# mLSTM row logits and mask by TensorE products, the maximum as a bias, the state's decay on ScalarE, and a phase barrier that TensorE passes

## The reference, cut to what matters

```python
bcum = cumsum(fc)
dmat = where(tril, bcum[t] - bcum[s] + it[s], -inf)
m_t  = maximum(bcum + m_prev, dmat.max(axis=-1))
w    = exp(dmat - m_t);  wqk = w * (q @ k.T);  a = exp(bcum + m_prev - m_t)
num  = wqk @ v + a * (c_prev @ q);  den = wqk.sum(-1) + a * (n_prev . q)
h    = num / maximum(abs(den), exp(-m_t))
m_new = maximum(b_last + m_prev, (b_last - bcum + it).max(-1))
decay = exp(b_last + m_prev - m_new);  ws = exp(b_last - bcum + it - m_new)
c_new = decay * c_prev + (ws * v).T @ k
```

## Time and profile before

| | |
|---|---|
| profiled execution, its own time | 3641.28 us |
| its span, first to last instruction | 3639.6 us |
| median of three runs | 3638.76 us |
| mean granted TensorE clock, share of 2.4 GHz | 0.937 |
| TensorE matmul busy | 3242.0 us (89%) |
| VectorE / ScalarE / GpSimd busy | 1779.0 / 1031.9 / 409.0 us |

### The profile page before, as it was taken

The page is one execution under the profiler, slowest core; times in us unless marked ns, Lnnn a source line. Parts: engine busy times, 40 slices in busy tenths (PEclk is TensorE's granted clock), DMA queues, the critical chain, the costliest instruction groups (busy, mean ns, idle before and its releaser), DMA issues. The chain is left out here.

```text
span 3639.6 us, 45789 instructions
## 1 busy us (share of the span) xinstructions
PE 3242.0 (89%) x17846; PEld 2901.8 (80%) x17846; DVE 1779.0 (49%) x3262; ACT 1031.9 (28%) x1632; POOL 409.0 (11%) x286
## 2 busy tenths in 40 slices
PE   6988899979999989599999868889979999879997
PEld 5978888868899789599999858667767797657875
DVE  6656445432346765764211374645523387443234
ACT  2221224323222442211211122124423324332221
POOL 0001200100010010321022020010000110121011
PEclk6999999979999999799999979999989999989998
DMA  5411320211042013342221233131221331232322
GB/s 189 156 38 37 86 93 24 83 51 53 24 163 87 24 70 116 108 124 75 71 69 44 90 122 95 44 107 59 70 64 53 114 124 35 95 114 83 108 81 98
DMA packets 332305, 303.73 MB, mean 83 GB/s; under 512 B 39822, under 2 KB 309852, under 8 KB 330204
## 3 DMA queue, kind: packets, MB, share of 16 engines
q1 hardware_dynamic: 315406, 229.74, 21.1%
q10 hardware_dynamic: 16718, 71.52, 5.3%
HBM read 266.47 MB, written 34.34 MB: 83 GB/s over the span
## 5 line engine op out<-in xcount | busy, mean ns | idle before, releaser
L741 PE MATMUL ps<-u_hi,w_hi 128*128 128x384 f32 (+1 forms) x2352 | 690.1, 355 | 61.4 <-ACTq L410 19.1
L741 PE MATMUL ps<-u_hi,w_lo 128*128 128x384 f32 (+1 forms) x2352 | 684.3, 353 | 0.0
L741 PE MATMUL ps<-u_lo,w_hi 128*128 128x384 f32 (+1 forms) x2352 | 683.9, 353 | 0.0
L1529 DVE TENSOR_TENSOR w_lo<-w_raw,w_hi 128x2048 fp32r<-128x2048 f32 x145 | 357.4, 2465 | 482.2 <-ACT w_hi L1135 481.0
L741 PEld LDWEIGHTS ps<-u_hi,w_hi 128*128 128x128 f32 x2352 | 435.6, 192 | 95.4 <-issue 43.4
L741 PEld LDWEIGHTS ps<-u_lo,w_hi 128*128 128x128 f32 x2352 | 437.5, 192 | 22.5
L741 PEld LDWEIGHTS ps<-u_hi,w_lo 128*128 128x128 f32 x2352 | 437.0, 191 | 22.8
L1135 ACT ACTIVATE w_hi<-w_raw 128x2048 fp32r<-128x2048 f32 x145 | 277.4, 1913 | 515.1 <-PE ps L741 295.3
L833 PE MATMUL ps<-u_hi,w_hi 128*128 128x384 f32 (+1 forms) x816 | 320.4, 393 | 4.5 <-ACT space L1278 3.5
L833 PE MATMUL ps<-u_hi,w_lo 128*128 128x384 f32 (+1 forms) x816 | 298.0, 365 | 0.0
L833 PE MATMUL ps<-u_lo,w_hi 128*128 128x384 f32 (+1 forms) x816 | 295.3, 362 | 0.0
(11 more groups left out here) (232 smaller groups left out, 4538.2 us busy)
## 6 DMA issues: line engine op xcount, KB each, us to landing
w_raw<-in_w_in SPq DMA_DIRECT2D x288, 256.0 KB, 4.1
space<-in_w_mod SPq DMA_DIRECT2D x48, 1024.0 KB, 5.5
w_raw<-in_w_gate_up SPq DMA_DIRECT2D x176, 256.0 KB, 4.0
w_raw<-in_w_down SPq DMA_DIRECT2D x96, 192.0 KB, 2.8
w_raw<-in_w_branch SPq DMA_DIRECT2D x64, 256.0 KB, 3.5
h_scratch<-space ACTq DMA_DIRECT2D x4, 3072.0 KB, 9.3
space<-h_scratch ACTq DMA_DIRECT2D x4, 3072.0 KB, 10.3
m_scratch<-space ACTq DMA_DIRECT2D x3, 3072.0 KB, 10.0
```

The lines of the kernel that those rows point to most:

```text
L741: last = nc.tensor.matmul(ps[:, 2 * (t % 2) + b, 0:a1 - a0], wv[w][:, k, j * P:(j + 1) * P], xx[:, k, a0:a1], start=(k == 0 and w == 0 and ...
L1529: V.tensor_tensor(w_lo[slot][:, :], w_raw[slot][:, :], w_hi[slot][:, :].bitcast(F32), ALU.subtract).then_inc(w_lo_done, 1)
```

## The change

`rows(k+1)` is now made of one bf16 product (identity by mask, 512 columns) and, for each head, a product whose stationary operand is the logit column broadcast to 128 columns and whose moving operand is the identity. Steps that want no output make no rows. The chunk's unmasked maximum, before a reduction over each step's rows, is made once a layer in `prep_b` by a transpose, a reduction, a diagonal and a product. ScalarE takes the exponential per head straight from PSUM with the negated maximum as bias. The decay of the state is four ScalarE copies with a scale. The key scale 128^-0.5 moves into the copy that moves b_k out of PSUM. At a phase's end the other three engines wait for each other and for TensorE, while TensorE waits only where the next phase is no `gemm`; a `down` group's products wait for the split hidden tiles instead.

```diff
             def end(self):
                 self.n += 1
-                self.eng.drain().then_inc(phase_end, 1)
-                self.eng.wait_ge(phase_end, 4 * self.n)
+                self.eng.drain().then_inc(others_end, 1)
+                self.eng.wait_ge(others_end, 3 * self.n)
+                self.eng.wait_ge(pe_end, self.n)
+            def end_products(self, onward):
+                self.n += 1
+                self.eng.drain().then_inc(pe_end, 1)
+                if not onward:
+                    self.eng.wait_ge(others_end, 3 * self.n)
...
                 for g in groups:
+                    if g.name.startswith("down"):
+                        pe.wait_ge(hid_split, g.h0)
...
-                def rows(k):
-                    i = n.lstm + k
-                    pe.wait_ge(m_diag, i + 1)
-                    if i:
-                        pe.wait_ge(m_arg, i)
-                    nc.tensor.matmul(ps[:, 0, :], ones[:, :], b_diag[i % 2].rearrange("p h n -> p (h n)"), start=True,
-                                     stop=True).then_inc(m_rows, 1)
+                def rows(k, w):
+                    d, ch, want, _ = steps[k]
+                    if not want:
+                        return
+                    if w:
+                        pe.wait_ge(m_w, w)
+                    nc.tensor.matmul(ps[:, 0, :], ident_b[:, :],
+                                     mask_b[:, d, :].unsqueeze(1).to_broadcast([P, HEADS, P]), start=True, stop=False)
+                    for h in range(HEADS):
+                        last = nc.tensor.matmul(ps[:, 0, h * P:(h + 1) * P],
+                                                r_in[:, d, ch, h:h + 1].to_broadcast([P, P]), ident[:, :],
+                                                start=False, stop=h == HEADS - 1)
+                    last.then_inc(m_rows, 1)
...
+                        pe.wait_ge(r_ready, 2 * l + 1)
+                        nc.tensor.transpose(ps[0:48, 2, 0:P], r_in[:, :].rearrange("p d t h -> p (d t h)"),
+                                            ident[:, :]).then_inc(r_turned, 1)
+                        pe.wait_ge(r_ready, 2 * l + 2)
+                        nc.tensor.matmul(ps[:, 3, 0:48], ones[0:48, :], r_diag[0:48, :], start=True,
+                                         stop=True).then_inc(r_spread, 1)
...
-                        act.wait_ge(m_dm, n.lstm_e + 1)
-                        A(b_w[i % 2], b_dm[i % 2], ACT.Exp).then_inc(m_w, 1)
+                        act.wait_ge(m_neg, n.lstm_e + 1)
+                        for h in range(HEADS):
+                            last = A(b_w[i % 2][:, h, :], ps[:, 0, h * P:(h + 1) * P], ACT.Exp,
+                                     bias=b_neg[i % 2][:, h:h + 1])
+                        last.then_inc(m_w, 1)
...
+                def decay(k):
+                    i, d = n.lstm + k, steps[k][0]
+                    act.wait_ge(m_ex, i + 1)
+                    if steps[k][2]:
+                        act.wait_ge(m_prod, n.lstm_w)
+                    if i:
+                        act.wait_ge(m_state, i)
+                    for h in range(HEADS):
+                        last = A(c_st[:, d, h, :], c_st[:, d, h, :], ACT.Copy, scale=b_ex[:, i % 2, 3, h:h + 1])
+                    last.then_inc(m_decay, 1)
...
                     fill_split(k)
+                    decay(k)
                     if counts[k]:
...
-                def diagonal(k):
-                    d, ch, _, _ = steps[k]
-                    V.tensor_tensor(b_diag[(n.lstm + k) % 2], ident[:, :].unsqueeze(1).to_broadcast([P, HEADS, P]),
-                                    bc(r_in[:, d, ch, :], P), ALU.mult).then_inc(m_diag, 1)
...
-                    dve.wait_ge(m_rows, i + 1)
-                    own.did(V.reduce_max(b_max[:, 0, :], rows, AX))
+                    own.wait()
                     if want:
-                        own.did(V.tensor_tensor(dm, rows, mask[:, d, :].unsqueeze(1).to_broadcast([P, HEADS, P]),
-                                                ALU.add))
-                        own.wait()
-                        own.did(V.reduce_max(b_max[:, 1, :], dm, AX))
+                        dve.wait_ge(m_rows, n.lstm_m + 1)
+                        own.did(V.reduce_max(b_max[:, 1, :], ps[:, 0, :].rearrange("p (h n) -> p h n", h=HEADS), AX))
+                        n.lstm_m += 1
+                    own.did(V.tensor_tensor(b_max[:, 3, :], r_max4[:, d, ch, :], m, ALU.max))
...
-                        V.tensor_tensor(dm, dm, bc(b_max[:, 2, :], P), ALU.subtract).then_inc(m_dm, 1)
+                        V.tensor_scalar(b_neg[i % 2], b_max[:, 2, :], -1.0, None, ALU.mult).then_inc(m_neg, 1)
...
-                    own.did(V.tensor_scalar(b_ws[:, :], ex[:, 2, :], HD ** -0.5, None, ALU.mult))
-                    own.wait()
...
-                    own.did(V.tensor_tensor(c_st[:, d], c_st[:, d], bc(ex[:, 3, :], HD + 1), ALU.mult))
...
+                    dve.wait_ge(m_decay, i + 1)
                     dve.wait_ge(m_dc, i + 1)
```

More of the change, by code:

```diff
@@ L327, in build @@
         B_TWO = words(8, 6 * BW).rearrange("p (r s h n) -> p r s h n", r=3, s=2, h=HEADS)
-        b_diag, b_dm, b_w = ([B_TWO[:, i, j] for j in range(2)] for i in range(3))
+        b_w = [B_TWO[:, 2, j] for j in range(2)]
+        b_small = words(8, 4 * BW)
+        r_top, r_diag, r_max = b_small[:, 0:1], b_small[:, 64:112], b_small[:, 128:176]
+        r_max4 = r_max.rearrange("p (d t h) -> p d t h", d=2, t=NT)
+        b_neg = [b_small[:, 192 + HEADS * j:192 + HEADS * (j + 1)] for j in range(2)]
         B_TMP = words(26, 2 * BW + 2 * HEADS * (HD + 1))
@@ L380, in build @@
         m_stored, m_loaded, gate_sig = sem("m_stored"), sem("m_loaded"), sem("gate_sig")
-        m_diag, m_rows, m_scores, m_keys = sem("m_diag"), sem("m_rows"), sem("m_scores"), sem("m_keys")
-        m_dm, m_w, m_arg, m_ex = sem("m_dm"), sem("m_w"), sem("m_arg"), sem("m_ex")
+        r_ready, r_turned, r_spread = sem("r_ready"), sem("r_turned"), sem("r_spread")
+        m_rows, m_scores, m_keys, m_decay = sem("m_rows"), sem("m_scores"), sem("m_keys"), sem("m_decay")
+        m_neg, m_w, m_arg, m_ex = sem("m_neg"), sem("m_w"), sem("m_arg"), sem("m_ex")
         m_wqk, m_wt, m_wts, m_kws = sem("m_wqk"), sem("m_wt"), sem("m_wts"), sem("m_kws")
@@ L989, in keys @@
                     last.then_inc(m_keys, 1)
-                rows(0)
+                rows(0, n.lstm_w)
                 scores(0)
@@ L998, in mlstm @@
                     if more:
-                        rows(k + 1)
+                        rows(k + 1, w + want)
                     fill(k, 0)
@@ L1118, in _ @@
                             n.tr += 1
-                ph.end()
+                onward = kind == "gemm" and index + 1 < len(phases) and phases[index + 1][0] == "gemm"
+                ph.end_products(onward)
         @block.scalar
@@ L1168, in gemm_unit @@
                         A(tile_at(dst_tile(g, it, s, j), g.lat), acc(t % 2, g.lat),
-                          ACT.Copy if g.kind == "copy" else ACT.Sigmoid).then_inc(acc_free[t % 2], 1)
+                          ACT.Copy if g.kind == "copy" else ACT.Sigmoid,
+                          scale=HD ** -0.5 if g.name == "b_k" else 1.0).then_inc(acc_free[t % 2], 1)
                     elif g.name in SQUARED:
@@ L1921, in maxima @@
                         own.did(V.tensor_tensor(b_max[:, 2, :], b_max[:, 1, :], m, ALU.max))
-                    own.did(V.tensor_tensor(b_max[:, 3, :], b_max[:, 0, :], m, ALU.max))
-                    own.wait()
-                    if want:
-                        V.tensor_tensor(dm, dm, bc(b_max[:, 2, :], P), ALU.subtract).then_inc(m_dm, 1)
+                        own.wait()
+                        V.tensor_scalar(b_neg[i % 2], b_max[:, 2, :], -1.0, None, ALU.mult).then_inc(m_neg, 1)
                         own.did(V.tensor_tensor(arg[:, 0, :], m, b_max[:, 2, :], ALU.subtract))
@@ L1939, in mlstm @@
                     weights, ex = b_w[i % 2].rearrange("p h n -> p (h n)"), b_ex[:, i % 2]
-                    if k + 1 < len(steps):
-                        diagonal(k + 1)
                     if want:
@@ L1944, in mlstm @@
                         dve.wait_ge(m_scores, w + 1)
-                        V.scalar_tensor_tensor(weights, ps[:, 1, :], HD ** -0.5, weights, ALU.mult,
-                                               ALU.mult).then_inc(m_wqk, 1)
+                        V.tensor_tensor(weights, ps[:, 1, :], weights, ALU.mult).then_inc(m_wqk, 1)
                     dve.wait_ge(m_ex, i + 1)
-                    own.did(V.tensor_scalar(b_ws[:, :], ex[:, 2, :], HD ** -0.5, None, ALU.mult))
-                    own.wait()
                     dve.wait_ge(m_keys, i + 1)
-                    V.tensor_tensor(b_kws, ps[:, 3, :].rearrange("p (h n) -> p h n", h=HEADS), bc(b_ws[:, :], P),
+                    V.tensor_tensor(b_kws, ps[:, 3, :].rearrange("p (h n) -> p h n", h=HEADS), bc(ex[:, 2, :], P),
```

(9 more changed lines are left out.)

12 lines of the change are left out of this document (6 added, 6 removed).

## The result

The changed kernel takes 3578.92 us (median of 4 runs, 3576.45 to 3582.47), against 3639.4 for the kernel before on the same chip (4 runs, 3634.82 to 3640.52): ratio 0.9836, 95% interval 0.9823 to 0.9848. It is 60.5 us faster, where 70 was forecast; the time lies inside the range, 9.9 us above the forecast of 3569. The two profiled executions are 3641.28 and 3579.07, 62.2 apart.

What follows compares the result with a forecast made beforehand. TensorE, busy nearly nine tenths of the span, was taken to bound the kernel. Savings of 18.7 + 22.5 + 15.7 + 13.0 = 69.9 us from 3641.3 gave 3571.4 profiled, about 3569 us median; range 3553 to 3598.

Steps and rivals of the forecast that it cites:

- The forecast case: Whole kernel: all summed gains arrive, 69.9 us saved, about 3569 us; chance 0.56.
- rows are dear: mLSTM row products on TensorE take 2.1 us a step instead of 1.04, losing 20 us: 3589; chance 0.08.
- ScalarE's queue becomes the bound: mLSTM steps: VectorE waits for late ScalarE decays ahead of the state's update, kernel slower, 3675 us; chance 0.02.
- the edit does more: Cheap rows (0.6 us), a short prep (1.6), no restart cost at barriers: 3557 us; chance 0.09.
- TensorE gives the barriers back: Dense phases: TensorE runs ahead but next weight splits are late, 15.7 + 7.9 us lost: 3593; chance 0.08.
- the clock does not come back: Short TensorE idle times, as in steps without fills, still lower its clock: 13 us lost, 3582; chance 0.15.
- the steps without fills: mLSTM layer 1, steps 4 and 9: weights' transposes still wait for VectorE, so gains are 0.9 and 1.1 us.
- a full step: mLSTM step: idle gap 1.87 us and L968's 0.97 go, new rows cost 1.04, net 1.80 us saved.
- layer 1, clock apart: Layer 1's mLSTM: start, steps and last step together save 22.5 us, without any clock gain.
- clock inside the mLSTM: Three falls of TensorE's clock in the two mLSTM layers, 1.7 us each, would go: 5.1 us.
- barriers, idle time: Fourteen TensorE waits between dense phases: ten shrink to 0.4 us each, four down places lose the barrier's hop; 15.7 us saved.
- clock at the barriers: After five of the ten barrier waits TensorE's lowered clock would no longer fall: 7.9 us saved.

Runs made afterwards that it cites:

- the mLSTM alone: The changed kernel with TensorE waiting at every barrier again, against the kernel before: 3597.57 us, ratio 0.9882.
- barrier alone: The kernel before with only the hunks that let TensorE pass the barriers, mLSTM as before: 3625.58 us, ratio 0.9954.
- the early diagonal: The kernel before with VectorE making the diagonal of step k+2 right behind the maxima of step k+1: 3606.08 us, ratio 0.9901.
- the down groups: The changed kernel with the first unit of each down group waiting for each hidden tile as it comes to it: 3559.36 us, ratio 0.9782.

## Why the prediction was right, and where its sum was off

**The forecast case came true.** Rows start without idle time behind the state's product, the ten waits are down to 0.3 each, and the kernel is 1.6% faster. Of the rivals, *rows are dear* fell (1.03 us a set), *ScalarE's queue becomes the bound* fell twice (decay back on VectorE, decay made 1.6 us later for 3.4 us in all), *the edit does more* fell, and *TensorE gives the barriers back* fell, but for d_q. What did happen is half of *the clock does not come back*: the 5.1 us inside the mLSTM came, most of the 7.9 at the barriers did not, and not because of the steps without fills that this rival named.

Term by term, against the two profiled executions (62.9 us of span; the forecast had 69.9):

| term | forecast | measured | from |
|---|---|---|---|
| a full step | 1.80 | 1.72 to 1.75 | starts, layer 0 |
| start of layer 0, prep and mLSTM | 0 | 0.01 | leads at gate sums and step 0 |
| start of layer 1 | 4.4 | 4.7 | the same |
| layer 0, clock apart | 18.7 | 18.0 | 19.65 less one fall of 1.66 |
| layer 1, clock apart | 22.5 | 22.0 | 25.39 less two of 1.7 |
| clock inside the mLSTM | 5.1 | 5.1 | three falls of 1.7 |
| mLSTM part, all | 46.3 | 44.8 | the mLSTM alone |
| barriers, idle time | 15.7 | 16.2 | idle time, barrier alone |
| clock at the barriers | 7.9 | -0.9 or 1.0 | busy time, barrier alone, or on top of the mLSTM's part |

**The mLSTM's terms held within 0.7 us each.** The net of a step was high by 0.07: the gap of 1.87 us and the row passes came out as worked out from the earlier trace rows. The bf16 product was put at 0.23 and took 0.22; the broadcast stationary operand costs what a dense one does, so L977 was the right row to take. The steps without fills also went as forecast: 1.1 forecast and 1.01 measured for the second in layer 1, 0.9 and 0.65 (2.35 less a fall of 1.7) for the first. The transposes (L1026) wait there, 1.07 and 1.34 us, for VectorE: that is the next wait, as named.

**The barriers' idle time held, by parts that cancel.** That 15.7 met 16.2 is in part luck. The restart cost 0.3, not 0.4, a place (1 us more won). The down places gave 0.05 each, not 0.25 (0.8 less): behind GpSimd's last split a semaphore is waited for nearly as long as the whole barrier was. At layer 1's d_q the limit that the earlier trace rows set is there, the 1.8 us that stand as the longest wait for w_lo; with the barrier alone it is 3.2.

**The step that failed is the clock at the barriers,** "with 0.4 I expect it not to fall. ... 7.9 in all". Its first half is right: behind the passed barriers the clock stays at 1.00 where it had been near 0.6. The sum is wrong, since it took each fall as a debt of the idle time before it, and all other falls as fixed. With the barrier alone, TensorE's busy time did not shrink at all (3242.0 to 3242.9): there were falls at idle times of 1.7 us that had been harmless, and d_q's fall came back at the next wait. Beside the mLSTM's part the passed barriers gave 1.0 us of busy time (3232.0 to 3231.0); by subtraction, 62.9 less 45.0 for the mLSTM and 16.2 of idle time at the barriers, it is 1.7. So some 1 to 2 of the 7.9 came. Whether the falls moved because of the edit is open: one of them lies ahead of the first passed barrier, and two profiles of the changed kernel differ in some of theirs.

This one term is most of the difference between the 69.9 forecast and the 62.2 measured from profile to profile. The other 2.3 us of the miss of 9.9 are the step from profile to median: the forecast took 2.5 off for it, and the changed kernel's profiled execution stood only 0.2 above its median.

**The Trainium skill's rule on multiplications.** The trace shows the four decays in 1.29 us on ScalarE and, in the kernel before, one instruction of 0.69 on VectorE, and the time is the same with either. The Trainium skill, ScalarE: Activation LUTs, Rules for kernel authors, sends multiplications to VectorE; on which engine is quicker at it the trace agrees, and here it makes no difference where the decay stands, because both engines wait for TensorE at that point (the update of the state in all 24 steps, with either).

## What to carry to other kernels

Look for the round trip before the amount of work: one tile made a step earlier on the same engine gave 36 us, and all the rest, with 69 us less work on that engine, gave 8.5 more, which is hardly clear of the noise. A wait for a whole group of tiles should be split by the order in which its reader takes them; four such waits of 3 us gave 19 us. Count the idle time that an edit removes in full, but the lower clock behind it as an upper bound: it came back with the early diagonal (9.2 us) and with the down groups (11.7), and not with the barriers (-0.9 of 7.9).

## What was not expected of the hardware

- The granted clock fell or did not fall behind the same idle time of 1.7 to 1.8 us (0.83 and 1.00 over ten microseconds). In three places it did the same in two profiles of one kernel, and over the same work from 100 to 116 us it did not (1.00 and 0.89).
- Removing four idle times of some 3 us gave back 11.7 us of busy time for 12.1 us of waits, with the same products.
- Eight ScalarE copies of 128x129 without a pointer operand take 1.63 us, 0.20 each; four scalings with one take 1.29, 0.32 each.
